# Triangular inverses of a hybrid recurrent step: compact masked halves, and products of two heads in column and row tiles

## The reference

```python
# mixer A, exact chunked form; c rows a chunk
amat = where(strict, beta * decay * (k @ k.T), 0.0)
sol  = triangular_solve(amat + eye(c), concat([beta * v, beta * exp(g) * k]),
                        left_side=True, lower=True, unit_diagonal=True)
# mixer B, row by row
def step(S, inp):                       # S (heads, 64, 64)
    r, w, k, v, a, b = inp
    sa = S @ a
    S = S * w + outer(sa, b) + outer(v, k)
    return S, S @ r
# both
o_a = rms_norm(o_a) * silu(z_a);  o_b = (group_norm(o_b) + bonus) * silu(g_b)
x = x + concat([o_a, o_b]) @ w_out0
```

## Time and profile before

| | |
|---|---|
| median of three runs | 2274.55 us |
| profiled execution: span (its own time is not listed) | 2267.6 us |
| busy TensorE matmul / weight load | 2018.1 / 1799.9 us (89% / 79%) |
| busy VectorE / ScalarE / GpSimd | 878.4 / 605.7 / 532.4 us |
| the eight prompt tiles of `phase_mix0` | 606.52 to 1284.54 us of the span |
| longest group of instructions | L1318 on GpSimd, 118 x 1325 ns and 59 x 1346 ns |
| Y, L1846 / Z of levels 1 to 5, L1858, matmuls | 154.8 / 118.8 us busy |

### The profile page before, as it was taken

One profiled execution on the slowest core, in us unless ns is written; L12 is line 12 of the kernel. 1 busy time (PEld: TensorE's weight loads), 2 busy tenths in 40 slices (PEclk: granted clock), 3 DMA queues, 4 the chain that ended last, 5 costly groups with the idle time before them and its releaser, 6 DMA issues. The chain is left out here.

```text
span 2267.6 us, 33912 instructions
## 1 busy us (share of the span) xinstructions
PE 2018.1 (89%) x13531; PEld 1799.9 (79%) x13531; DVE 878.4 (39%) x1457; ACT 605.7 (27%) x1144; POOL 532.4 (23%) x445
## 2 busy tenths in 40 slices
PE   3999949999599999999999888689999997899986
PEld 2799949888598888888888766479999997677764
DVE  4355524665435535535436433330011001444432
ACT  4344432333233223222233212232111110211101
POOL 2322021110255335334344310121112110100000
PEclk6999979999799999998999987699999998688887
DMA  4122130321431201201203201342212211623214
GB/s 128 31 78 77 50 110 27 98 90 57 151 101 43 71 29 51 69 28 51 67 17 83 56 13 33 87 134 87 86 40 79 75 59 37 190 81 92 88 47 43
DMA packets 192188, 160.55 MB, mean 71 GB/s; under 512 B 34562, under 2 KB 174059, under 8 KB 192088
## 3 DMA queue, kind: packets, MB, share of 16 engines
q1 hardware_dynamic: 192088, 159.12, 24.0%
HBM read 103.96 MB, written 55.14 MB: 70 GB/s over the span
## 5 line engine op out<-in xcount | busy, mean ns | idle before, releaser
L1318 POOL TENSOR_TENSOR c_m<-c_sc,c_lev 128x512 f32<-128x512 f32 (+1 forms) x118 | 155.1, 1325 | 46.6 <-DVE c_sc L1614 43.6
L1846 PEld LDWEIGHTS c_bank<-c_inv,c_m 128*128 128x128 f32 (+1 forms) x1200 | 149.8, 197 | 8.9 <-issue 8.7
L1846 PE MATMUL c_bank<-c_inv,c_m 128*128 128x64 f32 (+1 forms) x1200 | 154.8, 275 | 0.5
L1318 POOL TENSOR_TENSOR c_m<-c_nt,c_lev 128x512 f32<-128x512 f32 (+1 forms) x59 | 79.4, 1346 | 261.7 <-PE c_bank L1846 131.7
L1656 DVE TENSOR_TENSOR c_inv<-c_inv,c_bank 128x256 f32<-128x256 f32 (+1 forms) x126 | 51.0, 414 | 213.5 <-PE c_bank L1858 213.5
L1754 PE MATMUL c_bank<-c_wo,c_ot 128*128 128x512 f32 (+1 forms) x288 | 132.3, 615 | 0.5 <-ACT c_invt L1371 0.5
L2290 DVE SCALAR_TENSOR_TENSOR e_t<-e_t,e_bank 128x512 f32<-128x512 f32 (+1 forms) x20 | 12.7, 633 | 289.7 <-ACT e_t L2243 289.7
L85 PE MATMUL e_bank<-e_wp0h,e_xh 128*128 128x256 f32 x432 | 123.1, 285 | 1.8 <-issue 1.8
L87 PE MATMUL e_bank<-e_wp0h,e_xl 128*128 128x256 f32 x432 | 123.0, 285 | 0.0
L86 PE MATMUL e_bank<-e_wp0l,e_xh 128*128 128x256 f32 x432 | 122.9, 285 | 0.0
L85 PE MATMUL e_bank<-e_wp1h,e_xh 128*128 128x256 f32 x432 | 122.3, 283 | 0.0
(11 more groups left out here) (562 smaller groups left out, 5181.9 us busy)
## 6 DMA issues: line engine op xcount, KB each, us to landing
e_w<-in_w_in_dram SPq DMA_DIRECT2D x16, 1024.0 KB, 6.6
b_w<-in_w_in_dram SPq DMA_DIRECT2D x17, 512.0 KB, 6.4
scratch_rw<-b_x SPq DMA_DIRECT2D x16, 544.0 KB, 2.7
a_w<-in_w_in_dram SPq DMA_DIRECT2D x16, 512.0 KB, 5.8
c_rw<-scratch_rw SPq DMA_DIRECT2D x32, 256.0 KB, 3.0
scratch_qkv<-a_o SPq DMA_DIRECT2D x12, 544.0 KB, 4.5
e_xs<-scratch_xnT SPq DMA_DIRECT2D x8, 544.0 KB, 4.2
scratch_ql<-e_qb SPq DMA_DIRECT2D x8, 544.0 KB, 2.9
```

Source lines behind the costliest of these rows:

```text
L1318: pool.tensor_tensor(M[u][0:T, :, 0:T], src, bc(lev[0:T, l:l + 1, 0:T], [T, 4, T]), ALU.mult).then_inc(ev(f"m{u}"), 1)
L1846: mm = pe.matmul(packed(2 * u, l, T, T)[:, k], M[u][0:T, k, 0:T], half(X[u][0:T, k, :], l, T, 0), start=True, stop=True)
```

## The change

`lev` and `M` keep the late columns alone (64 for 128). For levels 1 to 5: Y of two heads goes to two 64-wide column tiles of one PSUM area (`y_at`); a new VectorE copy (`choose`) packs the late columns of `X` into `XS`, and one transpose of 128x128 serves two heads (`t_all`, copied by ScalarE into `XC`); Z takes its stationary operand and moving operand from 64 partitions, so two heads are two 64-row tiles, each with a PSUM bank of its own (`z_all`), and the subtraction is done in two operations a set. Level 1 now has the copy and the transposes too. Level 6 keeps the four full transposes (`turn`), with Y and Z on 64 columns and 64 rows. Level 0 writes late columns alone into a buffer of its own, `X1T`, which GpSimd fills with the identity at the head of the stage; VectorE waits for that (`first`) before the first tile. `restart` is no longer kept; `phase_mlstm_in` makes it anew. Two buffers are given other storage (`Q1`, `Rout`), and the counts of the waits follow; these and the samples tile's tail are left out below.

```diff
+PER_TILE = 2 * (LEVELS - 2) + 1
...
-lev = sb("lev", [P, LEVELS, P])
+lev = sb("lev", [P, LEVELS, P // 2])
...
-M = [sb(f"m{u}", [P, 4, P]) for u in range(3)]
+M = [sb(f"m{u}", [P, 4, P // 2]) for u in range(3)]
+X1T = [sb(f"first{u}", [P, 4, P]) for u in range(3)]
+XC = [y[:, 2:4, :] for y in Y]
+XS = [sb(f"invs{u}", [P, 4 * (P // 2)]) for u in range(3)]
...
-bank = [ctx.enter_context(nc.psum_tensor(f"c_bank{i}", [P, 512], F32)) for i in range(8)]
+both = [ctx.enter_context(nc.psum_tensor(f"c_banks{i}", [P, 2, 512], F32)) for i in range(4)]
+bank = [both[i // 2][:, i % 2, :] for i in range(8)]
...
-def packed(b, l, T, r):
-    return bank[b][0:r, :].rearrange("p (k c) -> p k c", k=4)[:, :, 0:T // 2].rearrange("p k (b h) -> p k b h", h=1 << l)
+def y_at(u, T, k):
+    r = slice((k % 2) * (T // 2), (k % 2 + 1) * (T // 2))
+    return y_all(u, T)[r, k // 2, :]
+def y_all(u, T):
+    return both[u][0:T, 0, 0:256].rearrange("p (q c) -> p q c", q=2)[:, :, 0:T // 2]
+def t_all(u, T):
+    return both[u][0:T, 1, 0:256].rearrange("p (q c) -> p q c", q=2)[:, :, 0:T]
+def z_all(u, T, e):
+    return both[u][0:T, e, 256:512].rearrange("p (q c) -> p q c", q=2)[:, :, 0:T // 2]
+def late(t, l, T):
+    return t.rearrange("p k (b u h) -> p k b u h", u=2, h=1 << l)[:, :, :, 1, :]
+def chosen(u, T):
+    return XS[u][0:T, 0:2 * T].rearrange("p (k c) -> p k c", k=4)
+def z_last(u):
+    return both[u][0:P // 2, 0, :].rearrange("p (a k c) -> p a k c", a=2, k=4)[:, 1, :, :]
+def y_last(u):
+    return both[u][P // 2:P, 0, :].rearrange("p (a k c) -> p a k c", a=2, k=4)[:, 0, :, :]
...
-    done(pool.memset(lev[:, l, :], 0.0))
-    v = lev[:, l, :].rearrange("s (b u t) -> s b u t", u=2, t=h)[:, :, 1, :]
+    v = lev[:, l, :].rearrange("s (b t) -> s b t", t=h)
...
+for u in range(3):
+    done(pool.tensor_copy(X1T[u][:, :, :], bc(K.ident[:, :].rearrange("p (a c) -> p a c", a=1), [P, 4, P])))
...
+pool.sem_inc(ev("first"), 1)
...
-pool.tensor_tensor(M[u][0:T, :, 0:T], src, bc(lev[0:T, l:l + 1, 0:T], [T, 4, T]),
-                   ALU.mult).then_inc(ev(f"m{u}"), 1)
+pool.tensor_tensor(M[u][0:T, :, 0:T // 2].rearrange("p k (b h) -> p k b h", h=1 << l), late(src, l, T),
+                   bc(lev[0:T, l:l + 1, 0:T // 2].rearrange("p k (b h) -> p k b h", h=1 << l),
+                      [T, 4, T >> (l + 1), 1 << l]), ALU.mult).then_inc(ev(f"m{u}"), 1)
...
 def turned(i, T, l, u):
...
-    act.wait_ge(ev(f"xt_mm{u}"), (LEVELS - 2) * i + l)
+    act.wait_ge(ev(f"xt_mm{u}"), (LEVELS - 1) * i + l)
+    act.activation(XC[u][0:T, :, 0:T], t_all(u, T), ACT.Copy).then_inc(ev(f"xt{u}"), 1)
+def turned_last(i, T, l, u):
+    act.wait_ge(ev(f"xt_mm{u}"), (LEVELS - 1) * i + l)
+    act.wait_ge(ev("w_mm" if u == 0 else "sa_mm"), i)
...
         else:
...
-            act.activation(Y[u][0:T, :, 0:T // 2], v4(b, T, T // 2), ACT.Copy).then_inc(ev(f"y{u}"), 1)
-            if l > 1:
-                turned(i, T, l - 1, u)
+            if l < LEVELS - 1:
+                act.activation(Y[u][0:T, 0:2, 0:T // 2], y_all(u, T), ACT.Copy).then_inc(ev(f"y{u}"), 1)
+                turned(i, T, l, u)
+            else:
+                act.activation(Y[u][P // 2:P, :, 0:P // 2], y_last(u), ACT.Copy).then_inc(ev(f"y{u}"), 1)
+                turned_last(i, T, l, u)
...
+dve.wait_ge(ev("first"), 1)
...
 for u in range(3):
...
-    dve.wait_ge(ev("w_mm" if u == 0 else "sa_mm"), i)
-    dve.tensor_tensor(XT[u][0:T, :, 0:T], bc(K.ident[0:T, 0:T].rearrange("p (a c) -> p a c", a=1), [T, 4, T]),
-                      M[u][0:T, :, 0:T], ALU.subtract).then_inc(ev(f"xt1_{u}"), 1)
+    dve.wait_ge(ev(f"x1mm{u}"), i)
+    dve.tensor_tensor(late(X1T[u][0:T, :, 0:T], 0, T), bc(late(K.ident[0:T, 0:T].rearrange("p (a c) -> p a c", a=1), 0, T),
+                                                          [T, 4, T // 2, 1]),
+                      M[u][0:T, :, 0:T // 2].rearrange("p k (b h) -> p k b h", h=1), ALU.subtract).then_inc(ev(f"xt1_{u}"), 1)
...
+def choose(u, l):
+    if l == 1:
+        dve.wait_ge(ev(f"xk{u}"), n)
+        dve.wait_ge(ev(f"xt_mm{u}"), (LEVELS - 1) * i)
+    else:
+        dve.wait_ge(ev(f"xd{u}"), PER_TILE * i + 2 * (l - 1))
+    dve.tensor_copy(chosen(u, T).rearrange("p k (b h) -> p k b h", h=1 << l),
+                    late(X[u][0:T, :, 0:T], l, T)).then_inc(ev(f"xs{u}"), 1)
+for u in range(3):
+    choose(u, 1)
...
         if l < LEVELS - 1:
-            if l == 1:
-                dve.wait_ge(ev(f"xk{u}"), n)
-            dve.wait_ge(ev(f"xd{u}"), (LEVELS - 1) * i + l - 1)
-            x = half(X[u][0:T, :, :], l, T, 0)
-            dve.tensor_tensor(x, x, packed(2 * u + 1, l, T, T), ALU.subtract).then_inc(ev(f"xd{u}"), 1)
+            for e in range(2):
+                x = half(X[u][0:T, e::2, :], l, T, 0)
+                z = z_all(u, T, e).rearrange("p k (b h) -> p k b h", h=1 << l)
+                dve.tensor_tensor(x, x, z, ALU.subtract).then_inc(ev(f"xd{u}"), 1)
+            if l + 1 < min(levels, LEVELS - 1):
+                choose(u, l + 1)
         else:
-            dve.wait_ge(ev(f"xt{u}"), (LEVELS - 2) * n)
-            xt = half(XT[u][0:P // 2, :, :], l, T, 1)
-            dve.tensor_tensor(xt, xt, packed(2 * u, l, T, P // 2), ALU.subtract).then_inc(ev(f"xd{u}"), 1)
+            dve.wait_ge(ev(f"xt{u}"), (LEVELS - 1) * n)
+            xt = XT[u][0:P // 2, :, P // 2:P]
+            dve.tensor_tensor(xt, xt, z_last(u), ALU.subtract).then_inc(ev(f"xd{u}"), 1)
...
     for k in range(4):
-        mm = pe.transpose(v4(2 * u, T, T)[:, k, :], XT[u][0:T, k, 0:T], K.ident[0:T, 0:T])
+        mm = pe.transpose(v4(2 * u, T, T)[:, k, :], X1T[u][0:T, k, 0:T], K.ident[0:T, 0:T])
...
+def turn(u):
+    for k in range(4):
+        mm = pe.transpose(v4(2 * u + 1, T, T)[:, k, :], X[u][0:T, k, 0:T], K.ident[0:T, 0:T])
+    mm.then_inc(ev(f"xt_mm{u}"), 1)
...
         else:
-            pe.wait_ge(ev(f"xd{u}"), (LEVELS - 1) * i + l - 1)
+            pe.wait_ge(ev(f"xd{u}"), PER_TILE * i + 2 * (l - 1))
...
-        for k in range(4):
-            mm = pe.matmul(packed(2 * u, l, T, T)[:, k], M[u][0:T, k, 0:T], half(X[u][0:T, k, :], l, T, 0), start=True, stop=True)
-        mm.then_inc(ev(f"ymm{u}"), 1)
-        if l > 1:
+        if l < LEVELS - 1:
             for k in range(4):
-                mm = pe.transpose(v4(2 * u + 1, T, T)[:, k, :], X[u][0:T, k, 0:T], K.ident[0:T, 0:T])
+                mm = pe.matmul(y_at(u, T, k), M[u][0:T, k, 0:T // 2], half(X[u][0:T, k, :], l, T, 0),
+                               start=True, stop=True)
+            mm.then_inc(ev(f"ymm{u}"), 1)
+            pe.wait_ge(ev(f"xs{u}"), (LEVELS - 2) * i + l)
+            for p in range(2):
+                mm = pe.transpose(t_all(u, T)[:, p, :], XS[u][0:T, p * T:(p + 1) * T], K.ident[0:T, 0:T])
...
+        else:
+            for k in range(4):
+                mm = pe.matmul(y_last(u)[:, k, :], M[u][:, k, 0:P // 2], X[u][:, k, 0:P // 2],
+                               start=True, stop=True)
+            mm.then_inc(ev(f"ymm{u}"), 1)
+            turn(u)
     for u in range(3):
...
-        if l > 1:
-            pe.wait_ge(ev(f"xt{u}"), (LEVELS - 2) * i + l - 1)
+        pe.wait_ge(ev(f"xt{u}"), (LEVELS - 1) * i + l)
+        if l == LEVELS - 1:
+            alone(pe, K)
         for k in range(4):
+            e, p = k % 2, k // 2
             if l < LEVELS - 1:
-                mm = pe.matmul(packed(2 * u + 1, l, T, T)[:, k], XT[u][0:T, k, 0:T], Y[u][0:T, k, 0:T // 2], start=True, stop=True)
+                r = slice(e * (T // 2), (e + 1) * (T // 2))
+                mm = pe.matmul(z_all(u, T, e)[:, p, :], XC[u][r, p, 0:T], Y[u][r, p, 0:T // 2],
+                               start=True, stop=True)
             else:
-                mm = pe.matmul(packed(2 * u, l, T, P // 2)[:, k], Y[u][0:T, k, 0:P // 2], half(XT[u][0:T, k, :], l, T, 1), start=True, stop=True)
+                mm = pe.matmul(z_last(u)[:, k, :], Y[u][P // 2:P, k, 0:P // 2], XT[u][P // 2:P, k, P // 2:P],
+                               start=True, stop=True)
...
 for x in X:
...
-done = Seq(ev("pseq"), pool, 4)
+done = Seq(ev("pseq"), pool, 7)
...
+done(pool.memset(restart[:, :], 1.0))
+done(pool.memset(restart[:, 0:SEQ:P], 0.0))
+done(pool.memset(restart[:, SEQ:TOK:DS], 0.0))
+pool.sem_inc(ev("restart"), 1)
```

More of the change, by code:

```diff
@@ L271 @@
           ("causal", [P, P]), ("strict", [P, P]), ("same", [SR, SR]), ("causal_s", [SR, SR]), ("strict_s", [SR, SR]),
-          ("last", [SR, SR]), ("restart", [P, TOK]), ("batch_cols", [P, DB, SR]),
+          ("last", [SR, SR]), ("batch_cols", [P, DB, SR]),
           ("head_cols", [P, 2]), ("lcausal", [P, P]), ("lcausal_s", [SR, SR]))
@@ L1269, in _ @@
             def _(pool):
-                done = Seq(ev("pool_seq"), pool, 8 + 4 * LEVELS)
+                done = Seq(ev("pool_seq"), pool, 8 + 3 * LEVELS + 3)
                 done.start(0)
@@ L1421, in tile @@
                         for u in range(3):
-                            turned(i, T, levels - 1, u)
```

(23 more changed lines are left out.)

4 lines of the change are left out of this document (2 added, 2 removed).

## The result

The changed kernel takes 2190.32 us (median of four runs, 2176.27 to 2192.39), the kernel before on the same chip 2273.24: a ratio of 0.963 with a 95% interval of 0.9587 to 0.9673. The forecast, 2225, had the sign and held the time in its range, but was 35 us too high; rival A's 2187 was nearer. The span of the profiled execution fell from 2267.6 to 2187.2 us, by 80.4 (its own time is 2189.03).

A forecast was written before the change was run, and what follows sets the result against it. TensorE's instructions were taken to bound the kernel until something else is late. Seven tiles -45, first tile -11.7 and +6.9, samples tile +1: -49 us on the 2267.6 span, 2218.5, plus 7 gives 2225; range 2180 to 2264.

The forecast's parts named there:

- rival A: Seven later tiles: the clock does not stay low after VectorE's long chain behind level 2; 2187 us, chance 0.2.
- up to level 2: Head and level 1 of a tile: halved masks and subtractions save 1.1, level 1 goes from 5.3 to 4.2; together 2.2 us.
- level 2 to the finished rows: Seven later tiles: this stretch 2.4 us shorter, despite level 3 waiting about 2.5 us for GpSimd's mask.
- the clock's: Seven later tiles: 1.2 GHz from the finished rows' transposes (L1744) until the projection, costing 5.5 us a tile.
- the gate: VectorE's five-operation chain after level 2, awaited by the finished rows' transposes: 5.0 for 7.4 us, those transposes 4.6 us earlier.
- change of shape: TensorE switching tile shape, seven times a level in levels 1 to 5: 0.2 us each.
- VectorE's chain: Subtractions and new copies in a level, 1.0 us a set; first Z to next first Z 4.2, just over TensorE's 4.1.
- The first tile: First of eight tiles: 11.7 us saved by shorter levels, 6.9 lost because VectorE waits for GpSimd's masks and three copies.
- B: VectorE's new copies wait behind GpSimd's masks: a level 5.2 instead of 4.2, 2244 us; chance 0.2.
- C: Levels 1 to 6 of every tile: TensorE streams less and its clock stays at 1.2 GHz; slower, 2349 us, chance 0.1.
- D: Levels 1 to 5: half-size tiles do not run two and two; a level 6.1, 2255 us, chance 0.05.
- 7 us put on the span: Whole kernel: the runs' median taken to lie 7 us over the profiled span, turning 2218.5 into 2225.

The follow-up runs named there:

- e2: The changed kernel with 20 unused transposes on TensorE ahead of level 3, filling its wait for GpSimd's masks; 2169.77 us, one run.
- e3: The changed kernel with GpSimd's power (norms) done after the masks of level 3 instead of before them; 2185.47 us, one run.
- e6: The changed kernel with Y of all three sets, then all transposes, then Z in levels 1 to 5: three shape changes instead of seven; 2190.89 us, one run.
- e4: The changed kernel with VectorE making each copy of the late columns twice; 2223.88 us, one run.
- e8: The changed kernel with GpSimd's power behind level 3's masks, VectorE's five operations spread over levels 2 to 4, finished rows and projections later; 2142.43 us, ratio 0.942.
- e5: The changed kernel with Z of levels 1 to 5 in runs of 12 instructions on one row tile, upper then lower; 2274.18 us, one run.

## Why the prediction was right, and where it was off

One tile by its own steps: starts in the trace of the tile of the earlier trace rows at 679.28, whose clock is 1.00 (level 2 at 702.27, the finished rows at 716.78, then 717.68, 724.16, 731.09 and 737.56, end 763.50), against the changed kernel's tile at 898.78 (919.06, 931.47, 933.37, 937.35, 944.41, 948.15, end 973.87).

| stretch | forecast | measured |
|---|---|---|
| up to level 2 | -2.2 | 22.99 to 20.28: -2.7 |
| level 2 to the finished rows | -2.4 | 14.51 to 12.41: -2.1 |
| finished rows | +0.7 | 0.90 to 1.90: +1.0 |
| level 4 | -2.4 + 3.7 | 6.48 to 3.98: -2.5 |
| first projection | +1.1 | 6.93 to 7.06: +0.1 |
| level 5 | -2.4 | 6.47 to 3.74: -2.7 |
| second projection, level 6 to the end | -0.3 | 25.94 to 25.72: -0.2 |
| tile | -4.2 | -9.1 |

**The step that failed** is the clock's: "so I expect 1.2 GHz in every one of the seven tiles from there until the projection ... 5.5". The fall came in every tile, as said, but neither where nor as long. I had 2.5 us of idle before level 3 and 1.8 after it, and took the fall to begin with the second. The second did not come about: the first one (2.24 measured) brought the fall in level 3 itself, level 3 ended later than the gate, and when level 4 began the clock was about to rise. Even at full clock it is 0.48 us and not 1.8 (e2): the gate ends earlier than I had it, 6.0 us earlier than before by the start of the finished rows in e2 where I took 4.6, and the masks of sets 1 and 2, 1.15 us each beside the gate, hold level 3 open. So level 4 and the projection, which I had charged 4.8, paid 0.3, and the fall cost 2.4 in all (e2). Seven times 4.9 are the 33 us that were missing (34.3, less 1.7, mostly of the last of these tiles, which is 1.5 longer than the others). The forecast's own scene, idle time ahead of the rows, is e3, where in five of the seven tiles level 4 and the projection do pay about what was forecast: in the one shown 6.5 us for 3.7 and 9.0 for 7.1, together 4.7 for 4.8.

**Sizes.** A level was 3.75, not 4.1 to 4.2: Y 0.38 a set with its change of shape (forecast 0.44), transposes 0.37 (0.42), Z 1.48 (1.53). A change of shape is 0.15 and not 0.2 (e6). VectorE's chain, put at 4.2, had 0.3 to 0.4 us of room (e4): its work is 0.73 a set where I took 1.0.

**The first tile** gained 9.0 where 11.7 - 6.9 = 4.8 was forecast. The late start was there, 4.3 us at level 1 for 6.9: GpSimd's three copies took 1.97 us, not 3.9. That nearest row (a mask with two inputs) was the wrong one for a copy; L560 of the earlier trace rows scaled to 512 columns, 0.49, would have been nearer to the 0.66 us of one copy.

**The rivals.** A gave 2187 for another reason than it happened: the clock did fall, only not in the expensive place, and the levels were faster than in its sum. B: one copy a tile, in level 1 beside a mask, takes 0.58 instead of 0.29 (916.15 above); there a copy does wait for GpSimd, as the rule of the Trainium skill (SBUF — State Buffer, Who interferes with whom) has it, but the others find GpSimd idle or meet it briefly (0.32 at most in the other copies of the eight tiles). So B is a matter of timing: where other edits put copies beside masks they paid its price (0.77 in e4's first tile, 0.80 in e8's level 4). C does not happen here; in e5's first tile, with most of Z's pairs lost, it does. D is refuted by e5; its 2255 is not worked out in the prediction.

The rest of the 35 us: 4.2 more from the first tile, 5.6 less outside these tiles (within what kernels with the same code there differ by), and 4 from the 7 us put on the span, since the median lies 3 over the span of the profiled execution now.

## What to carry to other kernels

When a change shortens the work of the engine that bounds, list what had been lying under that work (here a 2.28 us power ahead of a queue of masks): it is late next, and moving it behind the masks and spreading its users took the seven tiles from 527 to 491 us with no work taken away. Idle time on TensorE cost twice here, once as itself and once in the clock behind it, so ask not only whether the clock falls but which work stands where it is low. The half-size tiles of Z paid here only while two of them ran at once; with long runs on one tile the whole gain was lost (e5). And when a change takes one wait away, see whether the edit has put another in its place before dividing the gain by what was taken away (e6).

## What the runs showed of the hardware that I had not expected

- TensorE starts instructions for an idle row or column tile ahead of their turn: with four instructions of one tile in a row the pairs stayed (1.53 us for 24), with twelve eight of the 24 still overlapped (2.43).
- The clock fell without any idle time in the trace where TensorE was busy throughout, but for two thirds of Z worked on one row tile at a time (the first tile of e5: 637.40 to 646.90 at 1.00, then 0.50 for 30.7 us).
- A change of tile shape costs about 0.15 us by e6, where alternating pairs in the earlier trace rows had suggested 0.2.
